# Moving the sums of the up weights and of the activations from GpSimd to VectorE in a two-layer encoder kernel

## What is computed

```python
x = layer_norm(DEEPNORM_ALPHA * x + mix @ w_out[l], ln_g[l, 0], ln_b[l, 0])
hid = jnp.square(jax.nn.relu(x @ w_up[l]))          # 1024 -> 4096
x = layer_norm(DEEPNORM_ALPHA * x + hid @ w_down[l], ln_g[l, 1], ln_b[l, 1])
```

## Time and profile before

| | |
|---|---|
| median of 3 runs | 2842.94 us (2842.19 to 2845.5) |
| profiled execution | 2845.02 us, of which the span is 2843.2 us |
| PE busy | 2662.3 us (94%) |
| DVE busy | 1726.6 us (61%) |
| POOL busy | 1403.2 us (49%) |
| ACT busy | 1223.8 us (43%) |
| mean granted TensorE clock | 0.976 |

### The profile page before, as it was taken

How to read it: one execution, slowest core, us unless ns; L and a number is a source line. 1 busy time by engine, 2 the same in 40 slices (tenths; PEclk the granted TensorE clock), 3 DMA queues, 4 the chain that set the end, 5 groups by cost and what they waited for, 6 DMA issues and landing times.

```text
span 2843.2 us, 36920 instructions
## 1 busy us (share of the span) xinstructions
PE 2662.3 (94%) x12480; PEld 2060.2 (72%) x12480; DVE 1726.6 (61%) x3298; ACT 1223.8 (43%) x2463; POOL 1403.2 (49%) x1138
## 2 busy tenths in 40 slices
PE   8999999999989989899999999999999899898997
PEld 7787567678767767677877875676787677776776
DVE  3787876636683371733959877775376725518158
ACT  2575444332342533425335654443323435344343
POOL 5433600125676667767354345001266777576761
PEclk9999999999999999999999999999999999999999
DMA  5311335432522405023152132453325133240322
GB/s 155 83 49 45 85 72 111 116 115 89 167 92 106 146 19 204 30 106 113 53 142 57 45 80 46 93 117 89 133 83 185 63 134 118 102 146 5 138 81 78
DMA packets 117010, 276.67 MB, mean 97 GB/s; under 512 B 16186, under 2 KB 25338, under 8 KB 110394
## 3 DMA queue, kind: packets, MB, share of 16 engines
q1 hardware_dynamic: 107384, 248.99, 29.3%
q10 hardware_dynamic: 9440, 25.33, 2.4%
HBM read 194.67 MB, written 25.39 MB: 77 GB/s over the span
## 4 chain that ended last, share of the span: by engine, by line
PE 60%; DVE 14%; POOL 10%; issue 5%; DMA 4%; ACT 3%; SPq 2%; POOLq 0%; ACTq 0%; DVEq 0%
PE ps L1486 7%; POOL wlo L1229 5%; PE ps L1270 4%; POOL block L1197 4%; PE ps L1272 4%; PE ps L1271 4%; DVE hidden L2508 4%; PE ps L1672 3%; PE ps L1674 3%; PE ps L1673 3%; DVE x_place L2492 3%; PE ps L1641 2%; PE ps L1643 2%; PE ps L1642 2%; PE ps L1536 2%
## 5 line engine op out<-in xcount | busy, mean ns | idle before, releaser
L1229 POOL TENSOR_TENSOR wlo<-wraw,whi 128x512 fp32r<-128x512 f32 (+2 forms) x240 | 316.4, 1319 | 208.6 <-ACT whi L1738 195.7
L1227 POOL CAST whi<-wraw 128x512 fp32r<-128x512 f32 (+2 forms) x152 | 107.4, 707 | 600.2 <-DMA wraw<-in_w_out 288.3
L1229 POOL TENSOR_TENSOR wlo<-block,whi 128x512 fp32r<-128x512 f32 x240 | 314.3, 1313 | 162.4 <-ACT whi L1738 153.5
L1672 PE MATMUL ps<-whi,x_place 128*128 128x512 f32 x784 | 318.8, 407 | 64.3 <-DVE x_place L2492 54.4
L1738 ACT ACTIVATE whi<-block 128x512 fp32r<-128x512 f32 x240 | 150.1, 630 | 454.7 <-POOL block L1197 171.7
L1674 PE MATMUL ps<-whi,x_place 128*128 128x512 f32 x784 | 316.2, 403 | 0.0
L1673 PE MATMUL ps<-wlo,x_place 128*128 128x512 f32 x784 | 315.7, 403 | 0.0
L1882 ACT ACTIVATE probT<-ps 128x512 f32<-128x512 f32 (+2 forms) x456 | 204.9, 456 | 239.9 <-PE ps L1470 73.9
L2492 DVE TENSOR_TENSOR x_place<-hidden,x_place 128x512 fp32r<-128x512 f32 x196 | 203.8, 1081 | 141.7 <-ACT x_place L1964 140.5
L2528 DVE TENSOR_TENSOR hidden<-hidden,ps 128x512 f32<-128x512 f32 x72 | 49.4, 687 | 355.4 <-PE ps L1643 354.7
L1486 PE MATMUL ps<-probT,raw 128*65 128x512 f32 (+2 forms) x720 | 264.3, 450 | 0.0
(11 more groups left out here) (273 smaller groups left out, 6704.2 us busy)
## 6 DMA issues: line engine op xcount, KB each, us to landing
x_place<-x_sums SPq DMA_DIRECT2D x48, 1024.0 KB, 8.6
block<-in_w_up SPq DMA_DIRECT2D x120, 256.0 KB, 4.5
wraw<-in_w_in SPq DMA_DIRECT2D x80, 256.0 KB, 2.7
slot<-q_part SPq DMA_DIRECT2D x72, 256.0 KB
slot<-k_part SPq DMA_DIRECT2D x72, 256.0 KB
wraw<-in_w_out SPq DMA_DIRECT2D x64, 256.0 KB, 2.7
down_raw<-in_w_down SPq DMA_DIRECT2D x64, 256.0 KB, 5.7
wraw<-in_w_up SPq DMA_DIRECT2D x48, 256.0 KB, 2.8
```

The lines of the kernel that those rows point to most:

```text
L1229: nc.gpsimd.tensor_tensor(lo, loaded, hi.bitcast(F32), ALU.subtract).then_inc(S["w_lo"], 1)
L1672: mm(ps[:, bank, :], a, whi[j][:], start=(first and not more), stop=False, skip_group_check=more)
```

## The change

POOL keeps the rests of the weights and the sums T of w_down. It gives up the 16 block sums of w_up per pair stage and the 16 whole x blocks per layer; DVE makes them (`up_sums`, and four more instructions in each `x_differences`). The operand sums of the down stages are spread (`SUM_BESIDE`). Stores of the x sums, the loads of x halves and the next weights move in SP's list; ACT's list in the up part is reordered to match.

```diff
@@ block loads
-            if g:
-                for name in ("A11", "A12"):
-                    yield g + 1, name
-            for name in ("low odd", "high odd") if len(DOWNS[g]) > 1 else ():
+            for name in ("low odd", "high odd"):
                 yield g, name
-            if not g:
-                ...
-            for name in ("A21", "first A22"):
+            for name in ("A11", "A12", "A21", "first A22"):
                 yield g + 1, name
@@ sums_after(n), on POOL
     if kind == "pair":
         g, j = z
-        return {0: [("S1", g, k)], 1: [("S3", g, k)] + [("S2", g, 0)] * (k == 3), 2: [("S2", g, k + 1)] * (k < 3),
-                3: [("S4", g, k)], 4: [("T3" if k < 2 else "T1", DOWNS[g][0], k % 2)]}.get(j, [])
+        return [("T3" if k < 2 else "T1", DOWNS[g][0], k % 2)] if j == 4 else []
+UP_SUMS = [(name, g, k) for g in PAIRS for names in (("S1", "S3", "S2"), ("S4",)) for k in range(4) for name in names]
+HIDDEN_SUMS = [(c, at_) for cs in DOWNS for at_ in range(4) for c in cs]
+SUM_BESIDE = {2: {1: (0, 1), 2: (1, 1), 4: (0, 2), 5: (1, 2), 7: (0, 3), 8: (1, 3)}, 1: {0: (0, 2), 1: (0, 3)}}
@@ SP, up part of chunk 1
-                    if k == 5:
-                        save_x(0)
+                    if k in (1, 3, 5):
+                        save_x(k // 2)
@@ SP, load_pairs
-                save_x(1)
-                save_x(2)
-                sp.wait_ge(S["x_whole"], passed(l, "x_whole") + 16)
+                save_x(3)
                 ...
                 for g in PAIRS:
+                    if g > 1:
+                        load_block_of(g, "A11")
+                        load_block_of(g, "A12")
                     split_done(slab_product(DOWNS[g - 1][-1], N_PROD - 1) + 1)
                     load_block_of(g, "A21")
                     load_block_of(g, "first A22")
-                    for k in range(8):
-                        load_down(DOWNS[g][0], k)
                     load_x(g, t2, 0)
                     load_x(g, t2, 1)
                     load_x(g, t1, 0)
+                    for k in range(8):
+                        load_down(DOWNS[g][0], k)
+                    split_done(slab_pair(g, t2) + 3)
+                    sp.wait_ge(S["b_sum"], passed(l, "b_sum") + up_sum_count(("S4", g, 3)))
+                    load_block_of(g, "A22")
                     load_x(g, t1, 1)
                     load_x(g, t3_, 0)
-                    split_done(slab_pair(g, t2) + 3)
-                    sp.wait_ge(S["a_sum"], passed(l, "a_sum") + sum_count(("S4", g, 3)))
-                    load_block_of(g, "A22")
-                    ... (A11 and A12 of g + 1 between the x halves)
                     load_x(g, t3_, 1)
                     load_x(g, t4, 0)
                     load_x(g, t4, 1)
@@ ACT, up part
+            weights_hi(range(up1 - 4, up1 - 2))
             sums_hi(0)
+            weights_hi(range(up1 - 2, up1 + 2))
+            sums_hi(1)
+            weights_hi([up1 + 2])
             for m in range(4, 8):
                 relu(m)
             ...
@@ DVE, x_differences(k)
+                if k >= 2:
+                    dve.wait_ge(S[f"xt_saved{k % 2}"], passed(l, f"xt_saved{k % 2}") + 128)
+                for j, (k_tile, tok) in enumerate(((k, 0), (k, W), (4 + k, W), (4 + k, 0))):
+                    hi, lo = (z[:, k_tile, tok:tok + W].bitcast(F32) for z in (xhi, xlo))
+                    v_.tensor_tensor(t[j][:], hi, lo, ALU.add).then_inc(S["x_whole"], 1)
@@ DVE, new
+            def up_sums(g):
+                a11, a12, a21, a22 = (blocks[block_of(g, z)] for z in ("A11", "A12", "A21", "first A22"))
+                for z in ("A11", "A12", "A21", "first A22"):
+                    block = block_of(g, z)
+                    dve.wait_ge(block_loaded[block], 64 * (l * BLOCK_PER_LAYER[block] + block_count(g, z)))
+                for name, _, k in UP_SUMS[16 * (g - 1):16 * g]:
+                    if name in ("S2", "S4"):
+                        dve.wait_ge(S["w_lo"], slab_pair(g, 0 if name == "S2" else 1) + k + 1)
+                    dst, a, b, op = {"S1": (a22, a21, a22, ALU.add), "S3": (a21, a11, a21, ALU.subtract),
+                                     "S2": (a11, a22, a11, ALU.subtract), "S4": (a12, a12, a11, ALU.subtract)}[name]
+                    v_.tensor_tensor(dst[k][:], a[k][:], b[k][:], op).then_inc(S["b_sum"], 1)
+                    dve.wait_ge(S["b_sum"], passed(l, "b_sum") + up_sum_count((name, g, k)))
@@ DVE, down_sums(g)
                         operand_lo(next_c, next_q)
-                        if next_q == 2:
-                            s_sum(next_c, 2)
-                            s_sum(next_c, 3)
+                    if m in SUM_BESIDE[len(cs)]:
+                        z, at_ = SUM_BESIDE[len(cs)][m]
+                        s_sum(cs[z], at_)
@@ DVE, order of the stages
+            for k in range(4):
+                x_differences(k)
             operand_lo(0, 0)
             s_sum(0, 0)
-            s_sum(0, 1)
-            x_differences(3)
             operand_lo(1, 0)
             operand_lo(0, 1)
             s_sum(1, 0)
-            s_sum(1, 1)
             ...
             for g in PAIRS:
+                up_sums(g)
                 add_product(g, 0, 1, 0, even, 0)
                 ...
                 s_sum(even, 0)
-                s_sum(even, 1)
                 if len(DOWNS[g]) > 1:
                     ...
                     s_sum(odd, 0)
-                    s_sum(odd, 1)
                 else:
                     operand_lo(even, 1)
                     operand_lo(even, 2)
-                    s_sum(even, 2)
-                    s_sum(even, 3)
+                    s_sum(even, 1)
```

More of the change, by code:

```diff
@@ L421, in sum_count, with up_sum_count @@
     return SUM_ORDER.index(key) + 1
[L424 to L439 removed]
+UP_SUMS = [(name, g, k) for g in PAIRS for names in (("S1", "S3", "S2"), ("S4",)) for k in range(4) for name in names]
+def up_sum_count(key):
+    return UP_SUMS.index(key) + 1
+HIDDEN_SUMS = [(c, at_) for cs in DOWNS for at_ in range(4) for c in cs]
+SUM_BESIDE = {2: {1: (0, 1), 2: (1, 1), 4: (0, 2), 5: (1, 2), 7: (0, 3), 8: (1, 3)}, 1: {0: (0, 2), 1: (0, 3)}}
 PER_LAYER = {"bias_t_ready": 1, "bias_loaded": 16, "bias_t_loaded": 16, "thr_ready": 1, "signed": 1, "x_loaded": 16,
@@ L875, in weight_ready @@
                 else:
-                    engine.wait_ge(S["a_sum"], passed(l, "a_sum") + sum_count((name, g, k)))
+                    engine.wait_ge(S["b_sum"], passed(l, "b_sum") + up_sum_count((name, g, k)))
             elif kind == "product":
@@ L1052, in load_pairs @@
                 load_block_of(0, "high odd")
-                save_x(3)
                 for b in range(2):
@@ L1184, in difference @@
                 name, c, k = key
-                if name[0] == "T":
-                    b11, b12, b21, b22 = (raw_of(c, k, r, col) for r in range(2) for col in range(2))
-                    raw_loaded(pool, l, c, k)
-                    dst, a, b, op = {"T3": (t3[:, k], b22, b12, ALU.subtract), "T1": (b12, b12, b11, ALU.subtract),
-                                     "T2": (b11, b22, b12, ALU.subtract), "T4": (b21, b21, b11, ALU.subtract)}[name]
-                else:
-                    a11, a12, a21, a22 = (blocks[block_of(c, z)][k][:] for z in ("A11", "A12", "A21", "first A22"))
-                    for z in {"S1": ("A21", "first A22")}.get(name, ()):
-                        block = block_of(c, z)
-                        pool.wait_ge(block_loaded[block], 64 * (l * BLOCK_PER_LAYER[block] + block_count(c, z)))
-                    dst, a, b, op = {"S1": (a22, a21, a22, ALU.add), "S3": (a21, a11, a21, ALU.subtract),
-                                     "S2": (a11, a22, a11, ALU.subtract), "S4": (a12, a12, a11, ALU.subtract)}[name]
-                nc.gpsimd.tensor_tensor(dst, a, b, op).then_inc(S["a_sum"], 1)
-                pool.wait_ge(S["a_sum"], passed(l, "a_sum") + sum_count(key))
-            def whole(k, half):
-                if half == 0:
-                    if k == 0:
-                        pool.wait_ge(S["ln_done"], TILES)
-                        pool.wait_ge(S["t_lo"], 48)
-                    if k >= 2:
-                        pool.wait_ge(S[f"xt_saved{k % 2}"], passed(l, f"xt_saved{k % 2}") + 128)
-                for j in range(2 * half, 2 * half + 2):
-                    k_tile, tok = ((k, 0), (k, W), (4 + k, W), (4 + k, 0))[j]
-                    hi, lo = (z[:, k_tile, tok:tok + W].bitcast(F32) for z in (xhi, xlo))
-                    nc.gpsimd.tensor_tensor(xt[k % 2][j][:], hi, lo, ALU.add).then_inc(S["x_whole"], 1)
+                b11, b12, b21, b22 = (raw_of(c, k, r, col) for r in range(2) for col in range(2))
+                raw_loaded(pool, l, c, k)
+                dst, a, b = {"T3": (t3[:, k], b22, b12), "T1": (b12, b12, b11), "T2": (b11, b22, b12), "T4": (b21, b21, b11)}[name]
+                nc.gpsimd.tensor_tensor(dst, a, b, ALU.subtract).then_inc(S["a_sum"], 1)
```

(13 more changed lines are left out.)

35 lines of the change are left out of this document (6 added, 29 removed).

## The result

| | before | after |
|---|---|---|
| median, timed side by side on one chip | 2842.57 us (2837.87 to 2845.5, 4 runs) | 2728.99 us (2727.03 to 2731.91, 4 runs) |
| ratio of the times, 95% interval | | 0.9603 [0.9586, 0.9619] |
| profiled execution (span) | 2845.02 us (2843.2) | 2728.05 us (2726.3) |
| both MLPs | 1302.9 us | 1184.0 us |
| rest of the span | 1540.3 us | 1542.3 us |

The account below looks back on a forecast made before the run. TensorE was taken as the bound, with 144.8 us of MLP excess over its pace in both layers. With 23 us left, 121.8 us are gained from 2842.9: forecast 2721 us, likeliest range 2706 to 2735, 8 in 10 within 2704 to 2768.

Parts of the forecast that it names:

- up: MLP's up part: 1 us of excess left per layer (0 to 6) over the pace of 2.81 us a slab.
- down 0: First down stage: 5.2 us of excess left per layer (1 to 10), with POOL's rest and DVE late.
- three pair stages: Pair stages: 0.3 us of excess left in each (0 to 4), 0.9 per layer.
- down 1 and 2: Middle down stages: 1.6 us of excess left in each (0 to 6) behind POOL's chain, 3.2 per layer.
- down 3: Last down stage: one S sum moves behind the first PSUM sums, 3.4 us less; 1.2 us of excess left (0 to 4).
- sum: Excess left in a layer's MLP: 11.5 us, 23 in both layers, of 144.8 before; gain 121.8 us.
- The slack of 12 us (910 to 922): Pair stage 1: DVE's 16 sums end at 910 and may end as late as 922 before `add_product` is late.
- The rule on the shared port: Pair stages: one SBUF port locked between DVE and POOL leaves them as they are; 49 us less gain, 2770; chance 0.07.
- The DVE-bound down stages: Down stages: DVE stays the bound, about half of today's excess stays; 24 us less gain, 2745 us; chance 0.2.
- The full in-order DVE: Pair stages: sums ending past 922 hold up PE six times; 2871 us at 25 us past; chance 0.05.
- "The change doesn't do what it says": MLP: the stalls have another cause than DVE and POOL, so the same time, 2843 us; chance 0.03.

Follow-up runs that it names:

- experiment 1: The changed kernel with the old down-stage order on DVE: 2782.85 us; the kernel before with only the new down-stage order: 2786.73 us.
- 5: x_blocks_on_gpsimd: the changed kernel with the 16 x blocks back on POOL and the old SP, ACT and DVE places in the up part: 2745.29 us.
- experiment 3: The changed kernel with the 16 block sums of each pair stage back on POOL, the new load list kept: 2838.61 us.
- Experiment 6: The changed kernel with S1 of the last down stage made before the rests of q = 1 and q = 2: 2722.92 us.
- experiment 4: The changed kernel with extra DVE instructions ahead of each pair stage's 16 sums: 2733.62 us with 16 more, 2834.86 us with 40 more.
- old_load_order: The changed kernel with SP's old load list in the pair stages: 2729.28 us.
- delay_16: The changed kernel with 16 more DVE instructions (11.64 us) ahead of the 16 sums of each pair stage: 2733.62 us.
- delay_40: The changed kernel with 40 more DVE instructions (29.11 us) ahead of the 16 sums of each pair stage: 2834.86 us.

## Why the prediction was right, and where it was off

**The direction and the mechanisms** are shown. By stages the six pair stages took 520.7 us before and take 472.2 now, 48.5 less; the down stages won 59.3 and the up parts 11.1, which makes up the 118.9 us won in the MLPs. By causes the order in the down stages is worth 54 us taken out and 58 put in alone (experiment 1), the x blocks with their lists on SP and ACT 16 (5), and the block sums 44.5 with the order already in place (3). So about half of the gain is a new order on DVE, and not work moved from POOL.

**The sum by its terms**, excess over the pace per layer:

| term | forecast | measured |
|---|---|---|
| up | 1 | 0.1 |
| down 0 | 5.2 | 3.1 |
| three pair stages | 0.9 | -0.1 |
| down 1 and 2 | 3.2 | 3.5 |
| down 3 | 1.2 | 6.0 |
| sum | 11.5 | 12.6 |

The sum is close because errors of both signs met. The term that was mis-sized is down 3. S2 and S4 both moved behind the first additions, and S1 came in ahead of them: one S sum less there, as in "one of them moves behind, 3.4 us less". But the prediction didn't ask where S1 had stood before: in idle time, free. It came back ahead of `common` at 3.47 us, and PE's wait for `common` went from 4.1 us to 1.7 and not to nothing. The prediction also didn't follow the list to the end of the stage. The last product's rests were 4.28 us for four before, and take 6.62 now beside POOL, and PE waits 2.5 us for what is behind them. Experiment 6 gives 3.1 us a layer of this back with one line.

**The 8.0 us between 2721 and 2729.0:** 2.9 from the MLPs (118.9 for 121.8), 2.0 from the rest of the span, which was taken as unchanged, and 3.0 from how the profiled executions stand to their medians (2.1 above before, 0.9 below after). Of the 2.9, 0.7 are the window of layer 1 that began too early: the excess there was 70.6 us and not 71.3, and 144.1 in both layers. Of the 2.0, 1.8 are in the last stretch, behind the last MLP:

```profile
2664.00:2726.30 62.30, 46.26 (x192) 37.10 (x192) 48.21 (x82) 16.22 (x31) 2.51 (x2) 0.86 0.19 71
```

Before, it took 60.5 us with a clock of 0.91. The traces of the experiments show these two lengths again: 60.5 to 60.7 us in eight of the 13 kernels, 62.2 to 62.3 in five. x_blocks_on_gpsimd, which comes to this stretch through the same 45.4 us of down 3 and the same wait of 2.5 us as the change, is among the eight. So these 1.8 us are not shown to be an effect of the change; their cause is open.

**The pair stages** went as written: 78.7 us, 17.49 us for the sums, POOL's 33 or so instructions 44 us. The slack of 12 us (910 to 922) was near the measured one, for another reason: past some 10 us of delay the x half T1/1 is late first, and the large wait comes at S2 on the ninth slab, not at `add_product`'s bank (experiment 4).

**The rule on the shared port**, as a rival at 2770, is out: the pair stages lost nothing to DVE's sums, and PE's waits for `wlo` in them are gone. The Trainium skill's sentence ("Perfetto Trace Analysis", on moving work between the two engines) says that such a move might not help; here it did, by 44.5 us in the pair stages (experiment 3). The sums do feel POOL: 1.09 us each where the instruction takes 0.65 alone.

**The DVE-bound down stages**, as a rival at 2745, didn't come: no wait of PE for `operand_lo` above 2 us in sum is left. **The full in-order DVE**, slower than before, needs the sums more than 29 us late; with a delay of 29.1 the kernel is still 0.3% faster than before. **"The change doesn't do what it says"** is out by experiments 1, 3 and 5, which take its parts out and get the waits back.

## What to carry to other kernels

Moving work between two in-order engines paid here, though each slowed the other: the receiver idled 20.5 us in that very stage and does the instruction in half the time. Neither condition was varied by itself. Count the slack from the earliest reader behind all engines that the result passes through, not from the bank that looks tightest. For each instruction that an edit moves, look up where it stood before: one that sat in idle time is free, and put into the list that sets the time it costs nearly its full length (3.1 us of 3.47 here). A load order written around one sum is tied to the engine that makes it: it was worth nothing here with the fast engine, and cost 62 us with the slow one.

## What the runs showed of the hardware beyond that

- Sixteen DVE sums with two SBUF inputs took 17.49 us beside POOL at one instruction per slab. The delay's instruction, with one SBUF input, held 0.73 us each beside the same POOL work.
- Stalls of PE under 2 us in the down stages of the change left the granted clock at 1.00. Stages with stalls of 4 to 7 us had 0.93 to 0.96.
- A 1 MB load landed in 5.3 us in the median where it took 8.6, with no change to it. With SP's old list it took 7.2 (old_load_order), and with the new list and delayed sums 7.7 and 7.6 (delay_16, delay_40). So the time goes with the list and with when the sums are done; the two weren't taken apart.
